# Expert outputs summed in four PSUM banks by TensorE, with a ninth down slot and single banks elsewhere, in a two-layer mixer and expert kernel

## The reference, cut to what matters

```python
for l in range(DEPTH):
    h = rmsnorm(x, norm1_g[l])
    x = x + token_mixers(h, ...)
    h = rmsnorm(x, norm2_g[l])
    x = x + hierarchical_moe(h, ...)      # 1 of 4 groups, then 2 of its 8 experts, for each token
return rmsnorm(x, norm_f_g)

# in hierarchical_moe, for each of the 32 experts e:
a = einsum('td,edf->tef', tb, w_g)        # gate, 1024 x 256, 1 MB
u = einsum('td,edf->tef', tb, w_u)        # up,   1024 x 256, 1 MB
hh = silu(a) * u * cb[:, :, None]
out += einsum('tef,efd->td', hh, w_d)     # down, 256 x 1024, 1 MB
```

## Time and profile before

| | us |
|---|---|
| median of 3 runs (877.66 to 877.89) | 877.8 |
| the profiled execution, its own time | 877.06 |
| span of the profile, first to last instruction | 875.3 |
| TensorE busy | 817.2 (93%) |
| VectorE busy | 529.7 (61%) |
| ScalarE busy | 383.3 (44%) |
| mean DMA rate over the span | 322 GB/s |

### The profile page before, as it was taken

The page is one execution under the profiler, slowest core; times in us unless marked ns, Lnnn a source line. Parts: engine busy times, 40 slices in busy tenths (PEclk is TensorE's granted clock), DMA queues, the critical chain, the costliest instruction groups (busy, mean ns, idle before and its releaser), DMA issues.

```text
span 875.3 us, 20297 instructions
## 1 busy us (share of the span) xinstructions
PE 817.2 (93%) x8739; PEld 650.6 (74%) x8739; DVE 529.7 (61%) x1067; ACT 383.3 (44%) x653; POOL 117.5 (13%) x167
## 2 busy tenths in 40 slices
PE   7999999999999997877999999999999999986984
PEld 7898778888887775664589978787889766664652
DVE  5778898658555554423376788976656455543434
ACT  5546877545422221111275678764444222211113
POOL 2740102112000000000066001023200000000000
PEclk9999999999999999978999999999999999998888
DMA  9966454499979999999998463455996999999994
GB/s 303 389 237 167 172 184 154 144 411 359 368 295 420 418 420 419 420 420 420 401 370 309 157 220 131 169 193 229 393 353 275 422 419 419 418 419 421 420 420 183
DMA packets 64125, 281.47 MB, mean 322 GB/s; under 512 B 5120, under 2 KB 7248, under 8 KB 39712
## 3 DMA queue, kind: packets, MB, share of 16 engines
q1 hardware_dynamic: 62752, 278.45, 81.1%
q0 software_dynamic: 800, 1.40, 1.1%
q10 hardware_dynamic: 480, 0.28, 0.1%
HBM read 279.06 MB, written 1.05 MB: 320 GB/s over the span
## 4 chain that ended last, share of the span: by engine, by line
PE 72%; DMA 18%; SPq 6%; DVE 2%; ACT 1%; issue 1%; DVEq 0%; ACTq 0%
PE ps L491 15%; PE ps L493 14%; PE ps L492 14%; DMA ring<-in_w_exp_up 10%; PE ps L848 9%; DMA late<-in_w_exp_down 6%; PE ps L835 5%; PE ps L864 4%; SPq L381 4%; PE ps L947 3%; SPq L395 2%; DMA ring<-in_w_in 2%; PE ps L854 1%; PE ps L486 1%; PE ps L586 1%
## 5 line engine op out<-in xcount | busy, mean ns | idle before, releaser
L1689 DVE TENSOR_TENSOR split_lo<-ring,split_hi 128x1024 fp32r<-128x1024 f32 (+1 forms) x142 | 198.2, 1432 | 32.4 <-ACT split_hi L1168 31.3
L491 PE MATMUL ps<-split_hi,hT_hi 128*128 128x512 f32 (+2 forms) x416 | 161.6, 388 | 1.7 <-DVE hT_lo L1699 1.0
L1168 ACT ACTIVATE split_hi<-ring 128x1024 fp32r<-128x1024 f32 (+1 forms) x144 | 146.0, 1049 | 33.2 <-PE ps L493 31.0
L492 PE MATMUL ps<-split_lo,hT_hi 128*128 128x512 f32 (+2 forms) x416 | 157.7, 379 | 0.0
L493 PE MATMUL ps<-split_hi,hT_lo 128*128 128x512 f32 (+2 forms) x384 | 145.4, 379 | 0.0
L2105 DVE TENSOR_TENSOR wsT<-mb,ps 32x64 f32<-32x64 f32 x256 | 54.9, 214 | 141.4 <-ACT mb L1374 138.8
L1374 ACT ACTIVATE mb<-ps 128x64 f32<-128x64 f32 x64 | 14.3, 223 | 237.8 <-PE ps L848 237.8
L491 PEld LDWEIGHTS ps<-split_hi,hT_hi 128*128 128x128 f32 x416 | 78.2, 188 | 20.3 <-issue 4.7
L492 PEld LDWEIGHTS ps<-split_lo,hT_hi 128*128 128x128 f32 x416 | 78.4, 188 | 12.8
L493 PEld LDWEIGHTS ps<-split_hi,hT_lo 128*128 128x128 f32 x384 | 72.2, 188 | 13.1
L1593 POOL TENSOR_TENSOR idx<-idx,wt 128x128 f32<-128x128 f32 x32 | 12.1, 399 | 389.0 <-PE ps L870 307.3
(11 more groups left out here) (272 smaller groups left out, 1293.6 us busy)
## 6 DMA issues: line engine op xcount, KB each, us to landing
ring<-in_w_in SPq DMA_DIRECT2D x52, 1024.0 KB, 9.2
ring<-in_w_exp_gate SPq DMA_DIRECT2D x45, 1024.0 KB, 23.7
ring<-in_w_exp_up SPq DMA_DIRECT2D x45, 1024.0 KB, 26.0
late<-in_w_exp_down SPq DMA_DIRECT2D x38, 1024.0 KB, 26.5
ring<-in_w_exp_down SPq DMA_DIRECT2D x15, 1024.0 KB, 26.7
new_pair<-in_w_exp_gate SPq DMA_DIRECT2D x10, 1024.0 KB, 18.1
new_pair<-in_w_exp_up SPq DMA_DIRECT2D x10, 1024.0 KB, 20.2
late<-in_w_exp_gate SPq DMA_DIRECT2D x9, 1024.0 KB, 24.3
```

The costliest lines, as they stand in the source:

```text
L491: mm(dst, st[0], mv[0], start=start, stop=False, skip_group_check=True)
L492: mm(dst, st[0], mv[1], start=False, stop=False, skip_group_check=True)
L1168: A(half_view(split_hi[:, v % SPLITS, :], v), raw_half(v, l), ACT.Copy).then_inc(hi_done, 1)
L1689: V.tensor_tensor(half_view(split_lo[:, v % SPLITS, :], v), raw_half(v, l), half_view(split_hi[:, v % SPLITS, :], v).bitcast(F32), ALU.sub ...
```

## The change

Seven things change together.

1. x is copied by TensorE (`keep_x`, a product with the identity) into four PSUM banks (`ACC` = 4, 5, 6, 7) when an expert stage begins: six products in place of the eleven `keep_warm` products ahead of the rank products, and two in place of five behind them. All groups' scatters are then summed on top of it in these banks (`scatter_slots`, eight products of 256 columns in place of four of 512). `add_group` and its 56 additions are gone.
2. x in SBUF, 8 KB in each partition, is free during the expert stage and becomes a ninth down slot (`RD` = 9, name "x"). Its first load is that of expert 9. It waits for `x_kept` and for the two scaled copies of x (`xn_act`).
3. The other banks are single: 0 for gather and scatter matrices, 1 for transposes, 2 for gate and up, 3 for down. TensorE's order around expert e is now: transposes of e, gate and up of e + 1, down of e. Gate and up of e + 1 wait until VectorE has read those of e.
4. The gather of the next group is done in two halves, ahead of experts 0 and 1 of a group. The scatter moves from the second expert of a group to the third.
5. In `NEXT_LOADS` a pair stands 0 experts ahead of the down matrix at first, then 1 from expert 16 and 2 from expert 20 on (before: always 2).
6. At the end of layer 0 the four banks are copied to x (`take_quarter`) where they were added.
7. After layer 1 the last norm reads the sum out of PSUM; the eight additions are gone. ScalarE squares half a token tile, another half and the second tile; VectorE multiplies by the gain in between.

The diff, cut to its core:

```diff
+DOWNS = (("hT1", "hT0", "lo0", "lo1", 8, "yT", "att", "br", "x"),
+         ("att", 8, "br", "yT", "lo0", "lo1", "hT1", "hT0", "x"))
+RP, RD = 7, 9
+ACC = (4, 5, 6, 7)
...
+    _ahead = min(2, max(0, (_e - 12) // 4))
+    while _pair < min(NE, _e + _ahead + 1):
+        NEXT_LOADS.append(("gu", _pair))
+        _pair += 1
     NEXT_LOADS.append(("d", _e))
...
-                    keep_warm(11, 7)
+                    def keep_x(t, q):
+                        return mm(ps[:, ACC[q], T * t:T * t + T], ident[:], x[:, t, T * q:T * q + T],
+                                  start=(t == 0), stop=False, skip_group_check=True)
+                    for q in range(4):
+                        keep_x(0, q)
+                    for q in range(2):
+                        keep_x(1, q)
...
-                    keep_warm(5, 7)
+                    keep_x(1, 2)
+                    keep_x(1, 3).then_inc(x_kept, 1)
...
+                    def scatter_slots(y):
+                        for t in range(TT):
+                            for q in range(4):
+                                ins = mm(ps[:, ACC[q], 256 * t:256 * t + 256], scatT[:, t, :],
+                                         y[:, 256 * q:256 * q + 256], start=False, stop=True,
+                                         skip_group_check=True)
...
                     for e in range(NE):
                         g, i = e // GE, e % GE
-                        if i == 0 and g + 1 < GROUPS:
-                            gather_group(g + 1)
-                        if g >= 1 and i == (0 if g == GROUPS - 1 else 1):
-                            scatter_group(g - 1, (7, 0, 7, 0))
+                        if i < 2 and g + 1 < GROUPS:
+                            gather_group_half(g + 1, i)
+                        if g >= 1 and i == (0 if g == GROUPS - 1 else 2):
+                            scatter_group(g - 1)
...
-                        if e + 2 < NE:
-                            gate_up_expert(e + 2)
+                        hid_expert(e)
                         if e + 1 < NE:
-                            hid_expert(e + 1)
+                            gate_up_expert(e + 1)
                         down_expert(e)
                         if e > LASTG:
                             scatter_expert(e - 1)
...
+                        elif name == "x":
+                            sp.wait_ge(*L(xn_act, 2))
+                            sp.wait_ge(*L(x_kept, 1))
...
-                    for q in range(4):
-                        dve.wait_ge(tile_mm[q], 2 * l + 2)
-                        xs = x[:, t, 256 * q:256 * q + 256]
-                        ins = V.tensor_tensor(xs, xs, ps[:, ACC[q], 256 * t:256 * t + 256], ALU.add)
```

More of the change, by code:

```diff
@@ L825, in _, with gather_half @@
                         .then_inc(rank_mm, 1)
-                    keep_warm(5, 7)
[L829 to L839, removed]
+                    keep_x(1, 2)
+                    keep_x(1, 3).then_inc(x_kept, 1)
+                    def gather_half(b, bank_no):
+                        for c in range(4):
+                            cc = 4 * b + c
+                            for t in range(TT):
+                                ins = mm(ps[:, bank_no, P * c:P * c + P], wide[:, t, P * cc:P * cc + P],
+                                         pick[:, t, :], start=(t == 0), stop=(t == TT - 1), skip_group_check=True)
+                        return ins
                     def gate_up(w, hg, i, b, done, second_half=None):
@@ L938, in scatter_group @@
                         pe.wait_ge(*L(y_dve, GE * g + GE))
-                        if g >= 1:
-                            pe.wait_ge(*L(x_add, 4 * g))
-                        for k in range(4):
-                            t, hf = k // 2, k % 2
-                            if k == 1 and g + 2 < GROUPS:
-                                pe.wait_ge(*L(gath_out, 2 * (g + 2) + 1))
-                            if k >= 2:
-                                pe.wait_ge(*L(x_add, 4 * g + k - 1))
-                            mm(bank(banks[k]), scatT[:, t, :], y_slots[g % 2][:, 512 * hf:512 * hf + 512],
-                               start=True, stop=True).then_inc(scat_mm, 1)
+                        scatter_slots(y_slots[g % 2])
                     def hid_expert(e):
@@ L1012, in extra_pass @@
                     pe.wait_ge(x_y, 4 * n + 4)
-                    pe.wait_ge(x_scatT, n + 1)
-                    for k in range(4):
-                        t, hf = k // 2, k % 2
-                        ins = mm(bank((7, 0, 1, 4)[k]), scatT[:, t, :], y_slots[0][:, 512 * hf:512 * hf + 512],
-                                 start=True, stop=True)
-                    ins.then_inc(x_sc, 1)
+                    scatter_slots(y_slots[0]).then_inc(x_sc, 1)
                     pe.reg_add(extra, extra, 1)
@@ L1509, in _ @@
                         pool.wait_ge(x_out, l)
-                        pool.wait_ge(*last(x_add, 4 * GROUPS))
+                        pool.wait_ge(*last(x_add, 4))
                         layer_load(l)
@@ L2173, in extra_pass @@
                         dve.wait_ge(x_sc, n + 1)
-                        for k in range(4):
-                            t, hf = k // 2, k % 2
-                            xs = x[:, t, 512 * hf:512 * hf + 512]
-                            ins = V.tensor_tensor(xs, xs, bank((7, 0, 1, 4)[k]), ALU.add)
-                        ins.then_inc(x_sum, 1)
+                        V.memset(scal[:, 57:58], 0.0).then_inc(x_sum, 1)
                         dve.reg_add(extra, extra, 1)
```

241 lines of the change are left out of this document (122 added, 119 removed).

## The result

The changed kernel takes 883.73 us (median of 4 runs, 882.69 to 885.71) against 877.85 us for the kernel before in the same series (877.66 to 878.17): a ratio of 1.0066, with a 95% interval from 1.0054 to 1.0078. It is 5.9 us slower. The forecast was 875.5 us with a range from 873.4 to 880.6. The profiled execution took 884.75 us for a span of 883.0, and 883.0 - 875.3 = 7.7 us are to be found between the two traces.

What follows compares the result with a forecast made beforehand. The prediction took the weight loads to set the pace in the expert stages, between a gap and a tail. Its terms -5.0 + 4.3 - 0.5 - 1.1 = -2.3 us took 877.8 to 875.5 us, range 873.4 to 880.6.

Steps and rivals of the forecast that it cites:

- the tail: End of each expert stage, from down 29 to the last scatter: 9.75 us for 7.58, +2.17 in each layer, +4.3.
- Ninth slot: Load into x fills the DMA gap at the start of each expert stage: -2.50 us in each layer, -5.0.
- Rival E: Load into x misses the gap at the stage's start, so the 5.0 us are missing: 880.5 us; chance 6%.
- The stretch starts at once and stays full: Behind the gap, DMA engines don't run dry though the second and third pairs are issued later: cost 0.
- Single banks: Transposes wait for VectorE's product, 0.3 us an expert, hidden behind the loads: cost 0; without loads as bound, 19 us.
- Rival D: Single banks make TensorE the bound in the last two groups: 881.5 us if 3 us late in each layer; chance 8%.
- Additions: The 56 VectorE additions that go, 38.5 us busy, lay beside the loads: worth 0.
- Start of the experts: Products behind the rank products take 0.96 us for 1.20: -0.24 in each layer, -0.5.
- Last norm: After layer 1, from the last scatter to the end of the last square: 2.74 us for 3.85, -1.1.
- Rival C, the clock: TensorE's wait ahead of down 29 lowers its clock through the tail: 3.5 us over both layers, 879.0 us; chance 18%.
- Rival B: Layer 0's tail is free because the mixer's first weights set its start, 2.5 us sooner: 873.4 us; chance 8%.

Runs made afterwards that it cites:

- experiment 11: Changed kernel with one number of its load list changed: from expert 20 on a pair stands 1 expert ahead of the down matrix, not 2; 875.40 us.
- experiment 1: Changed kernel with the old order of work (gate and up two experts ahead), banks still single, ninth slot kept; 871.49 us.
- experiment 5: Kernel of experiment 1 without the ninth down slot; 876.69 us.
- experiment 3: Changed kernel without the ninth down slot (eight slots, no load into x); 890.32 us.
- Experiment 6: Changed kernel with 20 `keep_warm` calls ahead of the down product of expert 27 in each layer, filling the wait; 879.32 us.
- experiment 4: Kernel before with only the new list of loads (pairs 0, then 1, then 2 experts ahead of the down matrices); 877.4 us.
- experiment 7: Changed kernel with the old order of work (gate and up two experts ahead) from expert 24 on only; 874.17 us.
- experiment 12: Order of work of experiment 1 with the load list of experiment 11; 874.91 us.
- experiment 2: Changed kernel with gate and up of expert 31 and transposes of 30 and 31 put ahead of the down products of 29 and 30; 883.07 us.
- The runs with few bytes: A quarter of each gate and up matrix loaded from expert 7 on: changed kernel 822.15 us, kernel before 820.41, kernel of experiment 1 830.85.

## Why the prediction was wrong

**The step that failed** is the tail: "Before, from the down product of expert 29, which waits for its bytes, to the end it was 864.85 - 857.27 = 7.58 us", and the chain of 9.75 us counted from the same point for the changed kernel. I took it that down 29 would still wait for its bytes, so that the tail would start there. It waits for nothing (428.84, no bracket). The last wait for weights is that of down 27, and everything from 412.10 us on is the tail, 31.7 us where it was 21.5 from the same product: 10.2 us more, and the end of the stage 6.5 us later. The term was +2.17 in each layer. Counted as the prediction counts it, from the start of down 29 to the end of the last scatter, it is 15.0 us in layer 0 (428.84 to 443.80) and 10.9 in layer 1 (862.81 to 873.70), for 9.75. What the runs show in its place is two parts of the change that don't fit: item 3 halves the lead of gate and up in the work, from two experts to one, and item 5 keeps the lead of two experts in the list of loads at the end. TensorE waits for one matrix while two that it can't use yet have landed. I had costed item 3 against the earlier trace rows and item 5 not at all. Making them agree, by either of the two ways, takes off 8.3 or 12.2 us (experiments 11 and 1). At 875.4 us experiment 11 comes to where the forecast was; that is chance at least in part, as its last wait and its clock are not those that I counted.

**Ninth slot, -5.0: right.** The load into x is issued at 239.98 us, moves in the gap, and is worth 5.2 us in experiment 5. The bound that it can't be more than 2.50 us in a layer doesn't hold in the changed kernel, where it is 3.3 (experiment 3); why isn't shown. Rival E is out.

**The stretch starts at once and stays full, 0: a little off.** 416 for 419 GB/s over 80 us is 0.6 us in layer 0.

**Single banks, 0: right**, and the price without cover was put too high (21.3 us for a group, not 22 to 26, and 5.8 us in all, not 19). By the sum that leaves out the tail, experiment 1 with single banks should take 871.2 us, and it took 871.49. Rival D is out: its sign was a rate under 415 GB/s, and it is 416 in layer 0 and 420 from 760 to 855 us.

**Additions, 0: right as far as the stretch goes.** Nothing tells them apart from the rest.

**Start of the experts, -0.5.** The gather starts at 239.74 for 240.74 us and the first pair that waits for an expert is issued at 245.51 for 246.42. Behind the rank products it is 0.95 us (238.79 to 239.74) for 1.20, as forecast; the other 0.75 us are there before the rank products and what fills the time ahead of them begin (the products with x at L790 start at 228.41 us, those at L782 before at 229.16), so they come from the mixer. They lie inside the +6.5.

**Last norm, -1.1: right.** It measured -1.15.

**Rival C, the clock**, had the mechanism and not the place: I looked for it ahead of down 29, and it came at down 27 (a wait of 2.44 us, then a scatter of 5.81 for 3.69 us). Experiment 6 puts it near 4.4 us over both layers, where I had 3.5. Its sign, a clock under 1.00 in the last 10 us of a stage, came in layer 0 and not in layer 1 (1.00 from 863 to 873 us). The Trainium skill (TensorE: Matmul & The Clock Gate, Part 1) has clocks of 1.2 and 2.4 GHz; the 0.50 of the windows agrees.

**Rival B** is out: the mixer's first product waits for VectorE's hT_lo, now at 446.24 us as before at 439.70.

**One term more** had bounds that don't follow: the sum takes 3.8 to 4.8 us for both tails, and no row gives the 4.8; the bounds of the tail itself went up to 2.17 + 3.5 us.

**What stays open.** How the loss divides between the mismatch, the clock and the waits for issue. Experiment 6 prices the clock at one place. The waits for issue at the ends go with the order of work: none stands there in the kernel before and in experiments 1, 4, 5, 7 and 12, where gate and up run two ahead at the end, while 1.7 to 5.1 us over both layers do in the changed kernel and in experiments 2, 3, 6 and 11. No experiment changes them alone.

## What to carry to other kernels

When a change alters how far ahead work runs, lay the list of loads beside the list of work, load by load, at the end of the stage: a matrix that lands early there delays the one that is waited for, and here nothing behind it made that good. A tail begins at the last wait for bytes, so find that wait in the changed order first, instead of keeping the one that the old trace shows. Before calling an order good or bad, run it once with few bytes: here the order that is slower at TensorE's own pace is the faster one under the loads.

## What was not expected of the hardware

**TensorE stands still with its data there.** In the middle of a group of products, the profile shows waits for issue: 0.71, 1.75 and 0.39 us at the end of layer 0, 0.93, 0.93 and 0.36 at the end of layer 1, against 1.6 us in all in the expert stages of the kernel before. In experiment 1, with the same number of products, one of 2.18 us stands at 266.68 us and none at the ends. The row of the queue that carries instructions, on the page of the changed kernel:

```profile
q8 instruction: 72, 1.18, 0.5%
```

Its packets are 1.18 MB / 72 = 16 KB each. My reading, which isn't shown, is that TensorE waits for its own instructions, and that these come late because they share the DMA engines with the weights. The runs with few bytes speak for it in one case and against it in the other: the waits fall from 6.1 to 1.4 us in the changed kernel (822.15 us), and rise from 3.4 to 4.2 us with the old order of work (830.85 us). The cause stays open. The kernel before has 71 such packets, so it isn't their number.

**A short wait costs twice.** After 2.44 us without work down 27 took 1.73 for 1.07 us and the scatter behind it 5.81 for 3.69 us, so the clock was low for part of the time until 420.63 us. In experiment 1 a longer wait, of 3.89 us, was followed by 3.64 us of gate and up products at half clock, and the scatter behind them took its full-clock 3.69 us. The low clock fell on what stood behind the wait: on 16 down products, an idle microsecond and the scatter in the one case, on 64 gate and up products in the other.
